# Heads issued in pairs on the matrix engine, and a reordered last block, in a fused two-block transformer kernel

## The chip, the cores and the metric

The kernel runs as one program on one core of a Trainium2 chip. The metric is device time in microseconds (us), lower is better. TensorE (PE in the profile) multiplies matrices, VectorE (DVE), ScalarE (ACT) and GpSimd (POOL) work elementwise, SyncE (SP) starts the DMA transfers. The engines run side by side and meet only at semaphores. A wait stops everything behind it on its own engine.

## The reference, cut to what matters

512 tokens of width 1024 in float32 go through a first block of two layers, which is not touched, and then through a second block with four branches on the normalised input u:

```python
u = rms_norm(h, norm_mix_pre)
hq, hf, hi, hg, pz, sq, sk, sv, iq, ik, iw, mq = split(u @ w_in)
y_a = hgrn2_mixer(hq, hf, hi, hg, ...)   # gated recurrence, 4 heads, values 64 wide
y_b = pool_mixer(pz, ...)                # trailing-window means
y_c = dsa_mixer(sq, sk, sv, iq, ik, iw)  # indexer, top-128 keys, softmax attention
mk, mv = split(rms_norm(mem, norm_mem) @ w_mem_kv)
y_m = mem_attention(mq, mk, mv)          # 256 memory tokens, 4 heads
merged = sum(sigmoid(u @ w_gate[b]) * (y @ w_branch[b]) for b, y in branches)
h = h + rms_norm(merged @ w_out)         # then a gated feed-forward layer

# the indexer: 8 heads of width 64, weighted sum of relu over heads
logits = einsum('bqhd,bsd->bqsh', iq, ik) * 64 ** -0.5
score = einsum('bqsh,bqh->bqs', relu(logits), iw * 8 ** -0.5)
top_val, top_idx = top_k(score, 128)
```

## The kernel before, in words

Activations lie transposed in SBUF: 128 channels on the partitions, 512 tokens along the free dimension. A weight tile is a 1024 x 128 slice (8 blocks). It passes through four slots: SP loads it to RAW, ACT copies a rounded high part to WH (`hi_ahead`, L361), DVE or POOL writes the rest to WL (`lo_ahead`, `lo_one`, L377 and L367). Each dense product is then three matmuls per block (high x high, low x high, high x low; L397 to L399, in the last block also L1350 to L1352). High parts are made three tiles ahead of their use. Results of tiles alternate between PSUM banks 0 and 1, and PE may use a bank again once `evac` says it was read. A plain float32 matmul shows as two records.

All orders are written out by hand, one instruction list per engine. Four places matter here, all in the second block.

**Memory stage.** `second_pe` first makes memory keys (two tiles, `mem_kv(0)` and `mem_kv(1)`) and memory values (`mem_kv(2)`, `mem_kv(3)`), each 256 columns wide, through banks 0 and 1. PE then waits for both values to be read, and `lin_pair` runs the first two tiles of `w_in` block by block as the normalised input arrives. In `second_dve` the input blocks are scaled (L2553, `rn`) and their low parts made (L2556), ACT makes their high parts (L1942). The two values are read out (`mem_scaled`, L2539) and two weight tiles split between the first input blocks.

**Index loop.** 24 scores (3 query blocks x 8 heads, index r) of 64-row operands, 256, 384 and 512 keys wide (L1378). Even heads lie on partitions 0 to 63, odd heads on 64 to 127. Each goes to bank 2 or 3, ACT applies relu into PR (L1987), and DVE adds it into SC with its weight (L2636, L2639). After each score PE does one piece of filler: 3 matmuls of a gate tile, or after every 8 such pieces a branch product of 6 matmuls (`gated`, `branch_out`). After scores 8 and 17 ACT also handles a gate (`gate_act`: split, tanh, split), DVE after scores 9 and 18 a `merge`. Then DVE selects the top keys in 16 rounds (`select_round`) between further merges, which free banks for the gates and branches on PE.

**Sparse attention.** Eight steps of `pe_attend(("dsa",), ...)` with 11 pieces of 12 further tiles of `w_in` after each step. Step 7's softmax, the tiles' low parts (`LOWS`), the preparation of the recurrence on DVE (`hgrn_prepare`) and its logarithms on ACT (`hgrn_logs`) share the in-order queues. The result of the second pair of heads leaves bank 6 by ACT (`act_out`, L626) and DVE (`dve_out`, L633). Only then can `branch_out(2, 0)` run on PE.

**Recurrence.** Nine levels: DVE makes exponents (`decay`), ACT the exponential, DVE the scaled factors XX (`scale_by`), PE the products (L1431, L1440, L1449), DVE stores them into ATT (`keep`). PE fills with gate pieces. After the last level the values are applied (L1459, `hg_o`): head by head, into partition halves of one bank per pair of heads, 512, 384, 256 and 128 columns wide.

Of the kernel before, what the change touches and what calls it, by code (L numbers as in the profile page):

```python
# [18 lines left out]
P = 128  # L19
T = 512  # L20
D = 1024
DT = D // P
# [49 lines left out]
class Counts:  # L72
# [20 lines left out]
 asum ysum yt yo ot_in xt_in z r_tok merge os brf var_out var_in""".split()  # L93


def program(nc, known, t):
# [3 lines left out]
    with ctx:  # L100
# [758 lines left out]
        M_MQ = M_OUT + 4  # L859
# [316 lines left out]
        def _(pe):  # L1176
# [93 lines left out]
            def second_pe():  # L1270
# [19 lines left out]
                mem_kv(2)  # L1290
                mem_kv(3)
                evac_of(pe, M_MQ - 2)
                evac_of(pe, M_MQ - 1)
                lin_pair(XH, XL, ("r_hi", "r_lo"), "mixpre")
                turn("mv", MVT, 4)
# [77 lines left out]
                for r in range(24):  # L1373
                    qb, ih = r // 8 + 1, r % 8
                    rr = slice(ih % 2 * 64, ih % 2 * 64 + 64)
                    if r >= 2:
                        pe.wait_ge(sem["ixr"], cnt.value("ixr", r - 2))
                    x = pe.matmul(PB[2 + r % 2][:, 0:(qb + 1) * P], IQ[rr, ih // 2, qb * P:qb * P + P], IK2[rr, 0:(qb + 1) * P], start=True, stop=True)  # L1378
                    done(x, "ix", r)
                    next(fill)  # L1380
# [74 lines left out]
                for pr in range(2):  # L1455
                    for e in range(2):
                        h = 2 * pr + e
                        for a in range(TT):
# [305 lines left out]
        def _(act):  # L1764
# [164 lines left out]
            def second_act():  # L1929
# [8 lines left out]
                nxt()  # L1938
                rsqrt_act(act, "mixpre", D, EPS6)
                for j in range(DT):  # L1940
                    act.wait_ge(sem["rn"], cnt.value("rn", ("mixpre", j)))
                    done(act.activation(XH[:, j], ACC[:, j], ACT.Copy), "r_hi", ("mixpre", j))  # L1942
                    if j in (0, 1):
                        hi_ahead(act, st)
                        nxt()
# [23 lines left out]
                def gate_act(br, o):  # L1969
# [12 lines left out]
                    st.n += 1  # L1982
                for r in range(24):
# [21 lines left out]
                def dsa_between(c):  # L2005
                    for k in range(12):
# [22 lines left out]
                    if c == 7:  # L2029
                        hgrn_logs(14)  # L2030
# [203 lines left out]
        def _(dve):  # L2234
# [299 lines left out]
            def second_dve():  # L2534
# [15 lines left out]
                for j in range(DT + 1):  # L2550
# [6 lines left out]
                    if j in (0, 1):  # L2557
                        mem_scaled(MVT[:, j * NMEM:(j + 1) * NMEM])
# [99 lines left out]
                for c in range(2, 16):  # L2658
                    for _ in range(min(2 - c % 2, 16 - rnd)):
# [70 lines left out]
                LOWS = {0: (3,), 1: (4,), 2: (5,), 3: (6, 7), 4: (8,), 5: (9,), 6: (10, 11)}  # L2730
# [268 lines left out]
```

## Time and profile before

| | |
|---|---|
| median of 3 runs | 2342.56 us (2341.58 to 2343.31) |
| profiled execution | 2343.34 us, span 2341.3 us |
| PE busy | 2237.2 us (96%), mean granted clock 0.974 |
| DVE / ACT / POOL busy | 1244.0 (53%) / 888.9 (38%) / 345.5 us (15%) |

PE is a busy row because its matmuls overlap: a record of a 512-column matmul lasts 0.39 us while the next one starts 0.227 us later. So what PE can give back is seen in start times, in the granted clock and in idle times in brackets, not in the busy share. All times of rows are us from the span's start.

### The profile page before, as it was taken

Reading aid. Unit: us, or ns where it says so; the run is one execution under the profiler, and the core shown is the slowest. Engines: PE = TensorE matmul, PEld = TensorE weight load, DVE = VectorE, ACT = ScalarE, POOL = GpSimd, SP = SyncE. Lnnn points to the kernel's source line nnn. Section 1 sums busy time; section 2 is a strip of 40 time slices with the busy share of each in tenths; the row PEclk is TensorE's granted clock in tenths of the full one; section 3 lists DMA queues with packets and bytes.
Section 4 is the critical chain, followed back from the end, with each engine's and each line's share of the span. In section 5 each row is a group of like instructions: output and inputs, shape, how many; then the busy total and the mean of one; then the engine's idle time right before and its main releaser. Section 6 shows DMA issues by size and latency. Waiting matters only on the chain.

```text
span 2341.3 us, 27967 instructions
## 1 busy us (share of the span) xinstructions
PE 2237.2 (96%) x10174; PEld 1751.0 (75%) x10176; DVE 1244.0 (53%) x1936; ACT 888.9 (38%) x1463; POOL 345.5 (15%) x215
## 2 busy tenths in 40 slices
PE   7999899999999998899999989999989997999998
PEld 5767688888777776688888777568768775888886
DVE  4576643343554554643343575278589677443344
ACT  3545442242344553431342444322543343332333
POOL 0000600002410003400002510133023232000001
PEclk9999999999999999999999999779999998999999
DMA  5113233333232232233333333123222141323322
GB/s 165 24 44 93 64 100 110 89 96 99 72 110 73 73 99 64 72 102 104 90 99 99 90 100 83 32 64 102 74 59 73 48 115 55 99 85 112 90 73 71
DMA packets 368849, 196.90 MB, mean 84 GB/s; under 512 B 21072, under 2 KB 363869, under 8 KB 368750
## 3 DMA queue, kind: packets, MB, share of 16 engines
q1 hardware_dynamic: 368750, 195.58, 29.3%
q8 instruction: 62, 1.02, 0.2%
q14 instruction: 37, 0.30, 0.0%
HBM read 193.40 MB, written 2.14 MB: 84 GB/s over the span
## 4 chain that ended last, share of the span: by engine, by line
PE 86%; DVE 7%; ACT 3%; issue 2%; SPq 1%; DMA 0%; POOL 0%; DVEq 0%; ACTq 0%; POOLq 0%
PE PB L397 21%; PE PB L399 21%; PE PB L398 21%; PE PB L1350 3%; PE PB L1351 2%; PE PB L1352 2%; PE PB L480 2%; PE PB L526 2%; PE PB L499 2%; PE PB L1378 1%; PE PB L1431 1%; PE PB L1258 1%; PE PB L1259 1%; DVE WL L367 1%; PE PB L1264 1%
## 5 line engine op out<-in xcount | busy, mean ns | idle before, releaser
L361 ACT ACTIVATE WH<-RAW 128x1024 fp32r<-128x1024 f32 (+2 forms) x367 | 369.6, 1011 | 387.5 <-PE PB L399 359.5
L397 PE MATMUL PB<-XH,WH 128*128 128x512 f32 x1248 | 493.1, 395 | 12.7 <-DVE WL L367 6.6
L399 PE MATMUL PB<-XH,WL 128*128 128x512 f32 x1248 | 487.9, 391 | 0.0
L398 PE MATMUL PB<-XL,WH 128*128 128x512 f32 x1248 | 487.7, 391 | 0.0
L377 DVE TENSOR_TENSOR WL<-RAW,WH 128x1024 fp32r<-128x1024 f32 x192 | 252.6, 1316 | 187.2 <-ACT WH L361 177.0
L397 PEld LDWEIGHTS PB<-XH,WH 128*128 128x128 f32 x1248 | 235.1, 188 | 65.8 <-issue 12.4
L399 PEld LDWEIGHTS PB<-XH,WL 128*128 128x128 f32 x1248 | 235.0, 188 | 50.4
L398 PEld LDWEIGHTS PB<-XL,WH 128*128 128x128 f32 x1248 | 235.1, 188 | 47.9
L399 PE MATMUL PB<-HH,WL 128*128 128x512 f32 x512 | 199.2, 389 | 0.0
L397 PE MATMUL PB<-HH,WH 128*128 128x512 f32 x512 | 199.2, 389 | 0.0
L398 PE MATMUL PB<-HL,WH 128*128 128x512 f32 x512 | 199.2, 389 | 0.0
L367 DVE TENSOR_TENSOR WL<-RAW,WH 128x1024 fp32r<-128x1024 f32 (+3 forms) x135 | 167.0, 1240 | 58.2 <-ACT WH L361 57.8
L367 POOL TENSOR_TENSOR WL<-RAW,WH 128x1024 fp32r<-128x1024 f32 (+1 forms) x48 | 104.9, 2192 | 365.9 <-ACT WH L361 324.5
L765 POOL TENSOR_TENSOR SM<-ACC 128x512 f32<-128x512 f32 x4 | 5.2, 1292 | 895.9 <-DVE ACC L2409 530.8
L1871 ACT ACTIVATE HS<-HR 128x512 f32<-128x512 f32 x64 | 40.5, 632 | 195.2 <-DVE HR L2427 195.2
L613 ACT ACTIVATE PT<-PB 128x256 f32<-128x256 f32 (+3 forms) x160 | 65.4, 411 | 128.7 <-PE PB L499 128.7
L399 PEld LDWEIGHTS PB<-HH,WL 128*128 128x128 f32 x512 | 96.1, 188 | 20.1
L397 PEld LDWEIGHTS PB<-HH,WH 128*128 128x128 f32 x512 | 96.1, 188 | 19.9
L398 PEld LDWEIGHTS PB<-HL,WH 128*128 128x128 f32 x512 | 96.1, 188 | 19.8
L1350 PE MATMUL PB<-XH,WH 128*128 128x512 f32 x256 | 108.2, 423 | 1.0 <-ACT RS L1978 1.0
L1352 PE MATMUL PB<-XH,WL 128*128 128x512 f32 x256 | 103.6, 405 | 0.0
L1351 PE MATMUL PB<-XL,WH 128*128 128x512 f32 x256 | 103.6, 405 | 0.0
(506 smaller groups left out, 3624.8 us busy)
## 6 DMA issues: line engine op xcount, KB each, us to landing
RAW<-in_w_up SPq DMA_DIRECT2D x64, 512.0 KB, 4.1
RAW<-in_w_down SPq DMA_DIRECT2D x64, 512.0 KB, 3.8
RAW<-in_w_ffn_gate_up SPq DMA_DIRECT2D x44, 512.0 KB, 3.7
RAW<-in_w_gate SPq DMA_DIRECT2D x32, 512.0 KB, 3.9
RAW<-in_od_w_in SPq DMA_DIRECT2D x24, 512.0 KB, 6.2
RAW<-in_w_in SPq DMA_DIRECT2D x24, 512.0 KB, 3.7
RAW<-in_ple_w_gate SPq DMA_DIRECT2D x16, 512.0 KB, 4.0
RAW<-in_w_ffn_down SPq DMA_DIRECT2D x16, 512.0 KB, 3.8
```

Source lines behind the costliest of these rows:

```text
L361: act.activation(WH[:, s, 0:nb], RAW[:, s, 0:nb], ACT.Copy).then_inc(hi_done[s], 1)
L367: eng.tensor_tensor(WL[:, s, 0:nb], RAW[:, s, 0:nb], WH[:, s, 0:nb].bitcast(F32), ALU.subtract).then_inc(lo_done[s], 1)
L377: dve.tensor_tensor(WL[:, s], RAW[:, s], WH[:, s].bitcast(F32), ALU.subtract).then_inc(lo_done[s], 1)
L397: pe.matmul(PB[b][0:m, 0:n], WH[:, s, k, 0:m], rh[:, kk, :], start=kk == 0, stop=False)
L398: pe.matmul(PB[b][0:m, 0:n], WH[:, s, k, 0:m], rl[:, kk, :], start=False, stop=False)
L399: x = pe.matmul(PB[b][0:m, 0:n], WL[:, s, k, 0:m], rh[:, kk, :], start=False, stop=kk == last)
L480: xs[e] = pe.matmul(PB[2 + e][:, lo:lo + w], q[:, qb * P:qb * P + P], k[:, ks[0] * P:ks[0] * P + w], start=True, stop=plain)
L499: x = pe.transpose(PB[4 + e][:, c * P:c * P + P], PR[:, e, c * P:c * P + P], ID[:])
L613: done(act.activation(PT[:, e, ks[0]:ks[0] + len(ks), qb * P:qb * P + P], PB[4 + e][:, 0:len(ks) * P].rearrange("p (j q) -> p j q", q=P), ...
L1350: pe.matmul(PB[m % 2][:], WH[:, n % 4, k], XH[:, k], start=k == 0, stop=False)
L1351: pe.matmul(PB[m % 2][:], WH[:, n % 4, k], XL[:, k], start=False, stop=False)
L1352: x = pe.matmul(PB[m % 2][:], WL[:, n % 4, k], XH[:, k], start=False, stop=k == DT - 1)
```

## The change

It touches the second block alone. The memory values go into the two halves of PSUM bank 2 and DVE reads them in one instruction after the input blocks; PE waits for that (`mvt`) ahead of their transposition. Four splits of weight tiles move with it. The index loop issues two heads together, waits for both relus of the pair before, and runs two pieces of filler after them. In `hg_o` the two heads of a pair take turns block by block. The exp/tanh table is loaded ahead of the index loop and directly after the logarithms of step 5. The tanh of the recurrence moves ahead of the last copies out of step 7. The first merge after the index loop comes before the first selection rounds. Low parts of tiles 6 and 10 are made one step earlier, and the second `dve_out` comes before the first product of the recurrence.

```diff
--- before.py
+++ after.py
...
@@ -856,7 +856,7 @@
         M_IN = 2
         M_OUT = M_IN + 12 + 16 + 16 + 48 + 2 + 8
         M_OUT += 1 + 24 + 8 + 48 + 2 + 8
-        M_MQ = M_OUT + 4
+        M_MQ = M_OUT + 2
         M_GATE = {3: M_MQ + 12, 1: M_MQ + 28, 2: M_MQ + 56, 0: M_MQ + 72}
 
         def gate_bank(br, o):
@@ -1287,11 +1287,19 @@
                 mem_kv(0)
                 mem_kv(1)
                 pe_misc(pe, ("var", "mixpre"), x_squares)
-                mem_kv(2)
-                mem_kv(3)
-                evac_of(pe, M_MQ - 2)
-                evac_of(pe, M_MQ - 1)
+                pe.wait_ge(sem["pj_free"], cnt.value("pj_free", (1, 5)))
+                for c in range(2):
+                    s, u = st.slot(0)
+                    pe.wait_ge(lo_done[s], u + 1)
+                    into = PB[2][:, c * NMEM:(c + 1) * NMEM]
+                    for k in range(DT):
+                        pe.matmul(into, WH[:, s, k], MH[:, k], start=k == 0, stop=False)
+                        pe.matmul(into, WH[:, s, k], ML[:, k], start=False, stop=False)
+                        x = pe.matmul(into, WL[:, s, k], MH[:, k], start=False, stop=k == DT - 1)
+                    x.then_inc(used[s], 1)
+                    st.n += 1
                 lin_pair(XH, XL, ("r_hi", "r_lo"), "mixpre")
+                pe.wait_ge(sem["mvt"], cnt.value("mvt", 0))
                 turn("mv", MVT, 4)
                 for c in range(2):
                     lin1(8, XH, XL)
@@ -1370,13 +1378,17 @@
                 pe.wait_ge(sem["score_free"], cnt.value("score_free", 143))
                 pe.wait_ge(sem["score_free"], cnt.value("score_free", 142))
                 fill = itertools.chain(gated(3), gated(1))
-                for r in range(24):
-                    qb, ih = r // 8 + 1, r % 8
-                    rr = slice(ih % 2 * 64, ih % 2 * 64 + 64)
-                    if r >= 2:
-                        pe.wait_ge(sem["ixr"], cnt.value("ixr", r - 2))
-                    x = pe.matmul(PB[2 + r % 2][:, 0:(qb + 1) * P], IQ[rr, ih // 2, qb * P:qb * P + P], IK2[rr, 0:(qb + 1) * P], start=True, stop=True)
-                    done(x, "ix", r)
+                for pair in range(12):
+                    qb, it = pair // 4 + 1, pair % 4
+                    w = (qb + 1) * P
+                    if pair:
+                        pe.wait_ge(sem["ixr"], cnt.value("ixr", 2 * pair - 2))
+                        pe.wait_ge(sem["ixr"], cnt.value("ixr", 2 * pair - 1))
+                    for e in range(2):
+                        rr = slice(e * 64, e * 64 + 64)
+                        x = pe.matmul(PB[2 + e][:, 0:w], IQ[rr, it, qb * P:qb * P + P], IK2[rr, 0:w], start=True, stop=True)
+                        done(x, "ix", 2 * pair + e)
+                    next(fill)
                     next(fill)
                 for _ in fill:
                     pass
@@ -1453,9 +1465,9 @@
                 pe.wait_ge(sem["hg_read"], cnt.value("hg_read", q - 1))
                 pe.wait_ge(sem["misc_free"], cnt.value("misc_free", ("hv", 1)))
                 for pr in range(2):
-                    for e in range(2):
-                        h = 2 * pr + e
-                        for a in range(TT):
+                    for a in range(TT):
+                        for e in range(2):
+                            h = 2 * pr + e
                             x = pe.matmul(PB[6 - 4 * pr][e * 64:e * 64 + 64, a * P:T], HV[:, a, h * 64:h * 64 + 64],
                                           ATT[:, h, SLOT[a]:SLOT[a] + TT - a, :], start=a == 0, stop=a == TT - 1)
                     done(x, "hg_o", pr)
@@ -1936,13 +1948,14 @@
                 nxt()
                 hi_ahead(act, st)
                 nxt()
+                hi_ahead(act, st)
+                st.n += 1
                 rsqrt_act(act, "mixpre", D, EPS6)
+                hi_ahead(act, st)
+                st.n += 1
                 for j in range(DT):
                     act.wait_ge(sem["rn"], cnt.value("rn", ("mixpre", j)))
                     done(act.activation(XH[:, j], ACC[:, j], ACT.Copy), "r_hi", ("mixpre", j))
-                    if j in (0, 1):
-                        hi_ahead(act, st)
-                        nxt()
                 for c in range(2):
                     copy_out(MQ[:, c], scale=-0.125)
                 for c in range(2):
@@ -1980,6 +1993,7 @@
                         st.n += 1
                     hi_ahead(act, st)
                     st.n += 1
+                act.preload_act_table_set("exp_and_others")
                 for r in range(24):
                     w = (r // 8 + 2) * P
                     act.wait_ge(sem["ix"], cnt.value("ix", r))
@@ -2003,6 +2017,8 @@
                         done(act.activation(ACC[:, 0:4], ACC[:, 4:8], ACT.Tanh, scale=0.5), "hg_e", "tanh")
 
                 def dsa_between(c):
+                    if c == 7:
+                        hgrn_logs(14)
                     for k in range(12):
                         if (8 * k + 10) // 11 - 1 != c:
                             continue
@@ -2026,8 +2042,7 @@
                         done(act.activation(KK[:], KK[:], ACT.Exp, scale=-1.0), "hg_e", "inv")
                     if c == 5:
                         hgrn_logs(9)
-                    if c == 7:
-                        hgrn_logs(14)
+                        act.preload_act_table_set("exp_and_others")
                 act.preload_act_table_set(LN_TABLE)
                 act_attend(act, ("dsa",), 2, dsa_between, lambda: copy_out(ACC[:, 0]))
 
@@ -2554,8 +2569,15 @@
                     if j:
                         dve.wait_ge(sem["r_hi"], cnt.value("r_hi", ("mixpre", j - 1)))
                         done(dve.tensor_tensor(XL[:, j - 1], ACC[:, j - 1], XH[:, j - 1].bitcast(F32), ALU.subtract), "r_lo", ("mixpre", j - 1))
-                    if j in (0, 1):
-                        mem_scaled(MVT[:, j * NMEM:(j + 1) * NMEM])
+                    if j == 0:
+                        lo_ahead(dve, st)
+                        st.n += 1
+                lo_ahead(dve, st)
+                lin_ready(dve, st)
+                st.n += 1
+                twice = MRB[0][:].unsqueeze(1).to_broadcast([P, 2, NMEM])
+                halves_of = PB[2][:].rearrange("p (c n) -> p c n", n=NMEM)
+                done(dve.tensor_tensor(MVT[:].rearrange("p (c n) -> p c n", n=NMEM), halves_of, twice, ALU.mult), "mvt", 0)
                 for c in range(2):
                     skip()
                 dve.wait_ge(sem["misc"], cnt.value("misc", "mv"))
@@ -2656,7 +2678,7 @@
                     dve.wait_ge(sem["topk"], cnt.value("topk", (r, TT - 1, 1)))
                 rnd = 0
                 for c in range(2, 16):
-                    for _ in range(min(2 - c % 2, 16 - rnd)):
+                    for _ in range({2: 0, 3: 2}.get(c, min(2 - c % 2, 16 - rnd))):
                         select_round(rnd)
                         rnd += 1
                     merge(3 if c < DT else 1, c % DT)
@@ -2727,7 +2749,7 @@
                             for k in range(blk + n + 1, blk + 2 * n):
                                 link(dve.tensor_tensor(OFF[:, lv, :, k], OFF[:, 0, :, k - 1], OFF[:, lv, :, k - 1], ALU.add))
                 PREPARED = {3: (0,), 4: (1, 5), 5: (6, 7, 8), 6: (10, 11), 7: (14,)}
-                LOWS = {0: (3,), 1: (4,), 2: (5,), 3: (6, 7), 4: (8,), 5: (9,), 6: (10, 11)}
+                LOWS = {0: (3,), 1: (4,), 2: (5, 6), 3: (7,), 4: (8,), 5: (9, 10), 6: (11,)}
 
                 def dsa_between(c):
                     for n in LOWS.get(c, ()):
@@ -2741,8 +2763,8 @@
                         hgrn_prepare(12)
                         hgrn_prepare(13)
                 dve_attend(dve, ("dsa",), 2, dsa_between, last=False)
+                dve_out(dve, "dsa", 1)
                 dve.wait_ge(sem["hg_e"], cnt.value("hg_e", "tanh"))
-                dve.wait_ge(sem["pv"], cnt.value("pv", 19))
                 done(dve.scalar_tensor_tensor(QQ[:], ACC[:, 0:4], 1.0, ACC[:, 4:8], ALU.add, ALU.mult), "hg_small", "qk")
 
                 def halves(t_, lv):
@@ -2801,7 +2823,6 @@
                     done(x, "hg_read", q)
                     dve.wait_ge(sem["hg_read"], cnt.value("hg_read", q))
                 decay(0)
-                dve_out(dve, "dsa", 1)
                 for lv in range(9):
                     scale_by(lv)
                     if lv < 8:
```

## Rows read from the trace of the kernel before

**Rows 1.** The page, chain that ended last: shares of the span by engine.
```profile
PE 86%; DVE 7%; ACT 3%; issue 2%; SPq 1%; DMA 0%; POOL 0%; DVEq 0%; ACTq 0%; POOLq 0%
```

**Rows 2.** Stretches: us, busy us per engine (x instructions), PE clock, DMA share, GB/s.
```profile
1370.00:1404.00 34.00, 27.77 (x158) 24.03 (x157) 23.46 (x36) 15.02 (x21) 2.06 (x4) 0.90 0.31 85
...
1510.00:1520.00 10.00, 10.00 (x16) 3.99 (x15) 1.72 (x3) 1.58 (x3) 0.00 (x0) 0.50 0.01 2
...
1543.00:1560.00 17.00, 17.00 (x63) 13.46 (x63) 15.78 (x35) 5.26 (x7) 6.06 (x4) 0.84 0.16 46
...
1760.00:1800.00 40.00, 40.00 (x237) 35.32 (x236) 38.84 (x40) 15.10 (x14) 12.31 (x7) 1.00 0.24 66
```

**Rows 3.** Timeline of the memory stage: start, us, engine, line, [idle before <-releaser].
```profile
1383.45 0.75 DVE L2553 SCALAR_TENSOR_TENSOR ACC<-X,VEC,RS 128x512 f32<-128x512 f32 x1
...
1391.63 0.77 PE L1258 MATMUL PB<-XH,WH 128*128 128x512 f32 x1 [6.22 <-DVE MVT L2539]
...
1392.45 0.75 DVE L2553 SCALAR_TENSOR_TENSOR ACC<-X,VEC,RS 128x512 f32<-128x512 f32 x1
...
1393.71 0.75 DVE L2553 SCALAR_TENSOR_TENSOR ACC<-X,VEC,RS 128x512 f32<-128x512 f32 x1
...
1404.22 0.60 PE L1183 MATMUL PB<-ID,MVT 128*128 128x128 f32 x4
```

**Rows 4.** Timeline of PE in the index loop, 256 and 384 keys.
```profile
1480.74 0.70 PE L1378 MATMUL PB<-IK,IQ 64*128 64x256 f32 x2
...
1481.37 0.50 PE L1350 MATMUL PB<-XH,WH 128*128 128x512 f32 x1
...
1482.26 0.70 PE L1378 MATMUL PB<-IK,IQ 64*128 64x256 f32 x2
...
1491.38 0.91 PE L1378 MATMUL PB<-IK,IQ 64*128 64x384 f32 x2
...
1492.22 0.50 PE L1336 MATMUL PB<-YBH,WH 128*128 128x512 f32 x1
```

**Rows 5.** Timeline of PE at the index loop's end, 512 keys.
```profile
1541.17 2.07 PE L1378 MATMUL PB<-IK,IQ 64*128 64x512 f32 x2
1543.17 0.79 PE L1350 MATMUL PB<-XH,WH 128*128 128x512 f32 x1
```

**Rows 6.** Timeline of PE in the memory attention, scores of two heads together.
```profile
1428.96 0.70 PE L480 MATMUL PB<-MK,MQ 64*128 64x256 f32 x4
1429.60 0.66 PE L499 MATMUL PB<-ID,PR 128*128 128x128 f32 x4
```

**Rows 7.** Timeline of the index loop after score 9.
```profile
1493.78 1.28 ACT L1978 ACT_TABLE_LOAD   x1
...
1495.73 0.51 PE L1350 MATMUL PB<-XH,WH 128*128 128x512 f32 x1 [1.01 <-ACT RS L1978]
```

**Rows 8.** Timeline of the sparse attention's steps 6 and 7.
```profile
1706.34 1.90 ACT L2000 ACTIVATE FC<-FC 128x2048 f32<-128x2048 f32 x1
...
1712.32 0.66 PE L397 MATMUL PB<-XH,WH 128*128 128x512 f32 x1 [4.25 <-DVE WL L367]
...
1720.78 0.63 PE L1183 MATMUL PB<-ID,VT 128*128 128x128 f32 x4 [0.23 <-DVE HV L2739]
```

**Rows 9.** Timeline from the sparse attention into the recurrence.
```profile
1730.83 2.29 DVE L2746 SCALAR_TENSOR_TENSOR QQ<-ACC 128x2048 f32<-128x2048 f32 x1 [2.61 <-ACT ACC L2003]
...
1739.30 0.50 PE L1336 MATMUL PB<-YAH,WH 128*128 128x512 f32 x1 [4.46 <-DVE YAL L633]
...
1745.80 3.73 PE L1431 MATMUL PB<-XX 128*128 128x128 f32 x32
```

**Rows 10.** Timeline of PE after the recurrence's eighth level.
```profile
1823.26 2.02 PE L1440 MATMUL PB<-XX 128*128 128x128 f32 x16 [1.02 <-DVE ATT L2794]
```

**Rows 11.** Timeline of PE, values of the sparse attention, then of the recurrence.
```profile
1726.81 2.37 PE L526 MATMUL PB<-PT,SV 128*64 128x512 f32 x16
...
1840.95 7.05 PE L1459 MATMUL PB<-ATT,HV 128*64 128x512 f32 x32
```

More of the change, by code:

```diff
@@ L92 @@
  topk hsp hg_x hg_prod hg_read hg_e hg_d hg_o hg_small hx mn m2 varb ln_v x_full sum7q pj pj_free memsum cross xsum
- asum ysum yt yo ot_in xt_in z r_tok merge os brf var_out var_in""".split()
+ asum ysum mvt yt yo ot_in xt_in z r_tok merge os brf var_out var_in""".split()
 def program(nc, known, t):
```

## The prediction, made before the changed kernel was run

> **What bounds the kernel.** I read the chain of waits first: PE carries 86% of the path to the end [rows 1], so a gain must shorten PE's own work, raise its clock or close a hole in it. The stretches of the second block come next [rows 2]. In 1370 to 1404 PE is busy 27.77 of 34 us at a mean clock of 0.90: a hole. In 1510 to 1520 it is busy all the time at 0.50, that is at 1.2 instead of 2.4 GHz: a slow clock. In 1760 to 1800 PE shows 40.00 and DVE 38.84 busy us: two engines at their limit. The timelines of these places give the terms. The first block isn't touched, and elsewhere PE runs without holes, so a shift there is passed on rigidly.
>
> **Memory stage.** PE stands 6.22 us until DVE has read the second value tile, restarts at 1391.63 with a slow clock (0.77 us for a record) and reaches the transposition at 1404.22 [rows 3]. The change takes the values out of banks 0 and 1. What PE waits for next is the low part of the second `w_in` tile. DVE makes it straight after the first input block: 1383.45 + 0.75 + 1.23 (my reading of such a split; the table of groups has 1.24) = 1385.4. From there DVE gives one input block each 1.26 us (1392.45 to 1393.71), while PE needs six matmuls of 0.227 = 1.36 us per block; high parts come 1.4 us after the start of their scaling. PE takes four matmuls, waits 0.4 us for block 1 at 1386.75, and then is the limit: 7 x 1.36 + 0.45 = 10.0, end at 1396.75. DVE ends the eighth low part at 1395.1, splits one tile (1.2) and reads the values in one 512-wide instruction (0.7): 1397.0. So the new wait costs 0.25 us and the transposition starts at 1397.0 instead of 1404.22: **7.2 us**. Two moved splits on ACT fall into gaps (one ahead of the inverse root, one while DVE computes it); if one delays the first high part, it costs at most its 1.05 us. If PE were slowed through the whole pair I would lose the 48 matmuls' 0.2 us for about 3.4 us, some 1.7. I take 7.2, ends 4.5 and 8.
>
> **Index loop.** At full clock a 256-wide score takes 0.63 us of PE's time (1480.74 to 1481.37) and a piece of filler 0.89 (to 1482.26), of which 3 x 0.227 = 0.68 are matmuls and 0.21 the change of shape. At 384 it is 0.84, at 512 by the same step 1.05 [rows 4]. Two heads of the memory attention on the two row halves, also 256 wide, take 0.64 together [rows 6]: a second head is free. So a pair costs one score and two pieces cost 0.21 + 1.36 = 1.57: periods of 2.2, 2.4 and 2.6 us.
> Does the wait for both relus bind? After a pair ACT needs 0.1 + 0.5 + 0.6 = 1.2 to 1.35 us even at 512, under 1.57. DVE's two sums take 1.5 in a period of 2.6. It binds at two places. The table load of 1.28 us [rows 7] now stands before the first relu: PE waits 0.55. After score 8 ACT's split, tanh and split stand before relu 9. The second piece after that pair needs the tanh, 2.1 us after the pair, and PE is there at 1.57: 0.5, and again 0.3 for relu 9. Before, the hole at this place was 1.01 in PE and ended by the tanh behind the load [rows 7].
> Sum from the first score at 1479.22 (1480.74 less one period of 1.52): 2.8 + 3 x 2.2 + 3.95 + 3 x 2.4 + (1.05 + 0.21 + 0.68 + 1.36, with a branch product) + 3 x 2.6 = 31.7 us. Before, the last piece starts at 1543.17 [rows 5] and ends 1.45 later: 65.4 us. That is 33.7. Most is clock: a 512-wide score takes 2.00 us [rows 5] instead of 1.05, in a loop that stays at 0.50 [rows 2]. I assume the fall does not happen. It came after the hole of 1.01 us, in a loop where half of PE's rows idle in each score. The new loop uses all rows, and its period at 512 is 60% filler against 36 to 45%. After the loop the old kernel stays slow a little: 0.84 over 17 us [rows 2] is 5.4 us at 1.2 GHz, 3.8 of them after the loop, nine matmuls that lose 0.2 each: 1.8. Together **35.5 us**, ends 18 (slow clock, below) and 37.
> Selection: DVE is busy 15.78 of 17 us while PE never idles [rows 2]. The merge put before the first rounds frees the bank earlier, and the two rounds it displaces (3.1 us each) are caught up by the next merge, about 3 us before PE wants it. Nothing, at worst 1 us.
>
> **Sparse attention.** The low part of tile 10 leaves its place behind step 7's softmax, and the hole of 4.25 us before 1712.32 [rows 8] closes. But 1.15 us of splitting and 1.28 us of table load are now ahead of that softmax, behind logarithms that end at 1708.24 [rows 8]. Its probabilities come 2.4 us later. PE waits about 2 us for them, then for the next thing that is late: the second transposition of recurrence values needs DVE's copy of the first, which was the last waiter already (0.23 at 1720.78). That copy comes 2.4 later less the 1.15 of the split that left: 1.3 us later. The hole moves; it does not go. The values then end 1.3 us later, `dve_out` (0.7) comes next, and the first product of the recurrence starts near 1732.3 instead of 1730.83 [rows 9].
> Here the table load has two prices. In the row, 1.28 us, the next activation starts at once. The Trainium skill, "ScalarE: Activation LUTs", What ACT_TABLE_LOAD costs, adds 1.38 us of drain, 2.66 in all. By that rule each moved load would cost 1.4 more in its chain, and the sum would be some 2 us smaller. No drain is seen here, so the row's price stands in the sum.
>
> **Start of the recurrence.** The 4.46 us hole before 1739.30 [rows 9] ends because the low part of the output no longer waits behind two long DVE operations. PE reaches the first level's product near 1741, but the factors XX, before at 1743.0, now come 1.5 us later. From there DVE is full (38.84 of 40 [rows 2]), and at the eighth level PE waits 1.02 us for it [rows 10]. So PE's lead is lost and only DVE's start counts: minus 1.5, plus about 1 of DVE's waits for the late first product at 1745.80 [rows 9]. This stage together: **0.5 us lost**, ends 3 lost and 6 gained.
>
> **Recurrent values.** The same shapes for one pair of heads in turns are there: 16 records in 2.3 us. Head by head, 32 records take 7.05 [rows 11]. Two pairs in turns: 4.55. Everything to the end of the branch (sums of squares, roots, high and low parts) follows the last of these. **2.5 us**, ends 1.5 and 2.7.
>
> **Sum.** 7.2 + 35.5 - 0.5 + 2.5 = 44.7. From the profiled execution's 2343.34 us that gives 2298.6; its own time is 0.8 above the median of the runs, so 2298 us. Other edits (tile 6 one step earlier, tanh before copies) lie beside a PE without holes: nothing.
>
> **Rivals.**
> 1. The clock falls in the index loop all the same, say at the disturbed fifth pair, 13.4 us in. For it: the fall before came there, and the loop never recovered. Against: twice the rows in use, more filler. At half clock a pair takes 1.57, 2.00 and its filler 2.86: 3 x 4.4 + 6.1 + 3 x 4.9 = 34 us after the 13.4. The loop gives 18 instead of 33.7, the tail nothing: 44.7 - 17.5 = 27: 2316 us.
> 2. The pairs do not overlap, since scores here have other operands per half. Against: rows 6. Each pair then costs 0.43, 0.64 or 0.85 more, 4 of each: 7.7 us: 2306.
> 3. The sparse attention keeps what it closes (softmax earlier than I think, or DVE with slack in the levels): 6 more: 2292.
> 4. Slower than before: scores one after the other and a clock that is slow from the first pair, because 4 records of half the rows follow each other. Periods are then 5.1, 6.0 and 6.9, four of each, plus 2.6 for the branch products: 74.6 against 65.4. It decides from a mean clock of about 0.55 in the loop. Lost 9.2, with the memory stage's 7.2 back and nothing from the values: 2345.
> 5. The memory stage gives nothing, as PE waits for the one late read instead: 2305. It would need the input blocks to come 7 us later than computed.
>
> **Chances.** Forecast 0.72 (own range 2293 to 2303), rival 1 0.11, rival 2 0.04, rival 3 0.09, rival 4 0.02, rival 5 0.02. The range 2290 to 2312 takes in the unknown ends, rivals 2, 3 and 5 and a clock that falls late. About 0.2% (4.7 us) is what can be told from no change: faster 0.97, same 0.02, slower 0.01.
>
> **What would show it.** Memory stage: first `w_in` matmul near 1385.5, transposition near 1397, clock 1.00. Index loop: clock 1.00, pairs of four records in 0.64 to 1.05 us, 32 us in all. Step 7: PE holes near 2 and 3 to 4 us instead of 4.25; `branch_out(2, 0)` without a hole, a new one before the first level's product, DVE without waits through the levels. Values of the recurrence: 32 records in 4.5 us. The prediction is wrong if the loop's clock is below 0.9, or if PE's lead of the sparse attention survives the eighth level.

## The result and the profile after

| | before | after |
|---|---|---|
| median of runs (us) | 2342.32 (2341.58 to 2343.31, 4 runs) | 2306.80 (2303.79 to 2307.34, 4 runs) |
| ratio | | 0.9845, 95% interval 0.9828 to 0.9863 |
| profiled execution, its span | 2343.34, 2341.3 | 2307.16, 2305.1 |
| mean granted clock | 0.974 | 0.984 |

The change saves 35.5 us, where 44 were forecast. First the profile page's chain of waits, to be laid beside [rows 1]: PE has lost 2 points of the path, DVE has gained 1 and "issue" 2.

```profile
PE 84%; DVE 8%; issue 4%; ACT 3%; SPq 1%; DMA 0%; POOL 0%; DVEq 0%; ACTq 0%; POOLq 0%
```

Stretches of the kernel after, with the columns of [rows 2]. The memory stage has PE busy 33.80 of 34 us at clock 1.00 (27.77 at 0.90 before), the index loop runs at 1.00 where it was at 0.50. Behind a hole in the sparse attention the clock is 0.66. In the first levels of the recurrence DVE is busy 39.21 of 40 us and PE no longer 40.00 but 38.44.

```profile
1370.00:1404.00 34.00, 33.80 (x190) 28.54 (x189) 27.87 (x40) 18.31 (x25) 2.15 (x5) 1.00 0.41 112
1490.00:1500.00 10.00, 10.00 (x41) 5.66 (x39) 5.22 (x9) 5.52 (x10) 1.16 (x1) 1.00 0.19 54
1510.00:1520.00 10.00, 10.00 (x45) 8.26 (x45) 9.76 (x25) 2.61 (x3) 3.47 (x2) 1.00 0.26 79
1680.00:1690.00 10.00, 7.62 (x27) 6.32 (x28) 9.55 (x19) 3.86 (x4) 2.85 (x2) 0.66 0.05 13
1705.00:1745.00 40.00, 38.44 (x233) 33.96 (x234) 39.21 (x39) 14.90 (x14) 11.13 (x5) 1.00 0.17 48
```

Timeline of PE after, the starts that answer to [rows 3], [rows 7 to 11]: transposition of the memory values; a pair of scores at 256 keys (0.70 us for four records); the last pair, behind a hole; two holes that stand where one of 4.25 us was, and the slow restart behind the second; the first level; the eighth; the recurrent values, which begin at 1808.18.

```profile
1398.46 0.60 PE L1183 MATMUL PB<-ID,MVT 128*128 128x128 f32 x4
...
1478.58 0.70 PE L1389 MATMUL PB<-IK,IQ 64*128 64x256 f32 x4
...
1504.32 1.13 PE L1389 MATMUL PB<-IK,IQ 64*128 64x512 f32 x4 [1.42 <-ACT PR L2001]
...
1672.77 0.66 PE L499 MATMUL PB<-ID,PR 128*128 128x128 f32 x4 [1.09 <-DVE PR L604]
...
1682.38 1.09 PE L1183 MATMUL PB<-ID,VT 128*128 128x128 f32 x4 [5.83 <-DVE HV L2761]
1683.12 0.78 PE L397 MATMUL PB<-XH,WH 128*128 128x512 f32 x1
1683.70 0.63 PE L398 MATMUL PB<-XL,WH 128*128 128x512 f32 x1
...
1705.33 3.84 PE L1443 MATMUL PB<-XX 128*128 128x128 f32 x32 [2.08 <-DVE XX L2807]
...
1788.88 3.49 PE L1452 MATMUL PB<-XX 128*128 128x128 f32 x16 [1.92 <-DVE ATT L2816]
...
1808.18 4.53 PE L1471 MATMUL PB<-ATT,HV 128*64 128x512 f32 x32
```

Stage by stage, each as the distance between the same two instructions in both traces:

| from, to | before | after | gain | predicted |
|---|---|---|---|---|
| start, last untouched place before the memory stage | 1377.78 | 1379.42 | -1.6 | 0 |
| from there to the transposition | 26.44 | 19.04 | 7.4 | 7.2 |
| to the first index score | 75.00 | 75.07 | -0.1 | 0 |
| to the first sparse score (loop and tail) | 158.69 | 124.55 | 34.1 | 35.5 |
| sparse attention, to the second block of its values [rows 11] | 88.90 | 92.37 | -3.5 | } |
| to the first level's product | 18.99 | 14.88 | 4.1 | } -0.5 |
| to the eighth level's product | 77.46 | 83.55 | -6.1 | } |
| to the recurrent values | 17.69 | 19.30 | -1.6 | } |
| to the end | 500.35 | 496.92 | 3.4 | 2.5 |

The sum is 36.2, the difference of the spans. The first row is code that the change doesn't touch.

One pattern stands behind the 6.1 and 1.6 us lost in the levels. Timelines of DVE and then of POOL in the second and third level of the kernel after: DVE's subtraction, 1.23 us elsewhere, takes 3.29 us beside a split of POOL that reads two tiles from SBUF, and ends 1.08 us after it. XX at 1723.26 and 1725.24 is stretched in the same way.

```profile
1713.17 1.22 DVE L2807 TENSOR_TENSOR XX<-EE,QQ 128x1024 f32<-128x1024 f32 x1
1714.43 3.29 DVE L2784 TENSOR_TENSOR EE<-FC 128x1024 f32<-128x1024 f32 x1
1717.64 1.21 DVE L2785 TENSOR_TENSOR EE<-FC 128x1024 f32<-128x1024 f32 x1
...
1723.26 2.05 DVE L2806 TENSOR_TENSOR XX<-EE,KK 128x1024 f32<-128x1024 f32 x1
1725.24 2.31 DVE L2807 TENSOR_TENSOR XX<-EE,QQ 128x1024 f32<-128x1024 f32 x1
```
```profile
1713.83 2.81 POOL L367 TENSOR_TENSOR WL<-RAW,WH 128x1024 fp32r<-128x1024 f32 x1 [11.74 <-ACT WH L361]
1721.82 4.64 POOL L367 TENSOR_TENSOR WL<-RAW,WH 128x1024 fp32r<-128x1024 f32 x2 [5.19 <-ACT WH L361]
```

### The profile page after: what moved, and what is told of

Its sections match the earlier page's. It is cut to its first block, busy times and chain, and to the rows that moved or that the text cites. A ratio compares the mean times of both kernels' runs of the same rounds, so it can differ in the third digit from the quotient of the medians.

```text
span 2305.1 us, 27976 instructions
## 1 busy us (share of the span) xinstructions
PE 2201.5 (96%) x10174; PEld 1738.3 (75%) x10176; DVE 1251.2 (54%) x1935; ACT 888.0 (39%) x1463; POOL 347.6 (15%) x215
## 4 chain that ended last, share of the span: by engine, by line
PE 84%; DVE 8%; issue 4%; ACT 3%; SPq 1%; DMA 0%; POOL 0%; DVEq 0%; ACTq 0%; POOLq 0%
PE PB L397 22%; PE PB L399 21%; PE PB L398 21%; PE PB L480 2%; PE PB L526 2%; PE PB L1358 2%; PE PB L1360 2%; PE PB L1359 2%; PE PB L499 2%; DVE ATT L2816 1%; PE PB L1258 1%; PE PB L1259 1%; PE PB L1264 1%; DVE XX L2807 1%; PE PB L1344 0%
## 5 line engine op out<-in xcount | busy, mean ns | idle before, releaser
L398 PE MATMUL PB<-XL,WH 128*128 128x512 f32 x1248 | 488.2, 391 | 0.0
L2444 DVE TENSOR_TENSOR HL<-HS,HH 128x512 f32 x64 | 44.3, 692 | 106.9 <-ACT HH L1885 106.9
```

The lines of the kernel that those rows point to most:

```text
L398: pe.matmul(PB[b][0:m, 0:n], WH[:, s, k, 0:m], rl[:, kk, :], start=False, stop=False)
```

## The experiments

Times are medians; "after" is 2306.8, and each run stands beside runs of the kernel before on its own chip (36 of them in four batches, 2338.3 to 2346.5, medians of the batches 2342.5 to 2343.4). Executions of one kernel lie 1 to 7 us apart where the clock does not differ. Part of that arises ahead of the first edit: the last untouched place before the memory stage is reached between 1376.7 and 1380.4 us in the traces. So differences of 2 us between two kernels say little.

### What made the clock fall in the index loop

**Scores one by one, early table load kept.**
```
-for pair in range(12): ...        (two heads, two fillers)
+for r in range(24):               (one head, one filler)
+    if r >= 2: pe.wait_ge(sem["ixr"], cnt.value("ixr", r - 2))
```


> The changed kernel with its index scores one by one again, a wait and one filler piece behind each; all else as changed, the early table load too. Theory: a score of half of PE's rows between single pieces of filler brings the clock to 1.2 GHz by itself, with or without the hole of 1.01 us: the loop's granted clock falls to 0.50 to 0.60, the loop takes about 63 us instead of 32, and the time is 30 to 34 us above the changed kernel's, about 2338. Rival: the hole alone set off the fall, and the early load takes it away: the clock stays near 1.00; 12 further scores at full clock (4 each of 0.63, 0.84, 1.05) are 10 us, so about 2317.


Measured 2317.66 (2316.17 to 2318.59), ratio to before 0.9891 [0.9876, 0.9906]. My theory fell, the rival's number came: half-row scores between single fillers, with no hole among them, kept the clock at 1.00 in this trace. The pairing alone is worth 10.9 us by the medians and 9.6 in the traces' stage of loop and tail (134.10 against 124.55), which the rival worked out as 12 scores that no longer take time, 10 us.

**The kernel before with the early table load only.**
```
+act.preload_act_table_set("exp_and_others")
 for r in range(24):
```


> The kernel before with one edit, the exp table loaded ahead of its index loop. Theory: the hole of 1.01 us before 1495.73 goes, the clock falls all the same to 0.50 some us later, since scores and filler are the same; time within 3 us of before (2342). Rival: the hole was what set off the fall: clock near 1.00 through the loop, 25 to 30 us faster, about 2315.


Measured 2326.78 (2326.48 to 2328.06), 0.9932 [0.9916, 0.9947]: 16 us faster by one instruction that moved. The clock did what the rival said, the time lies between the two numbers. Stretches of this trace: the clock is 1.00 where it was 0.50 [rows 2], and falls only behind a new hole.

```profile
1510.00:1520.00 10.00, 10.00 (x29) 4.47 (x28) 6.34 (x7) 4.47 (x7) 2.38 (x1) 1.00 0.18 52
1520.00:1530.00 10.00, 10.00 (x40) 7.08 (x39) 7.47 (x13) 3.26 (x5) 3.70 (x2) 1.00 0.15 44
1530.00:1540.00 10.00, 6.59 (x22) 4.93 (x22) 9.83 (x25) 2.60 (x3) 1.80 (x1) 0.83 0.11 34
```
The hole, in this trace's timeline of PE, with the record at 0.63 instead of 0.39 us behind it:

```profile
1534.97 0.50 PE L1336 MATMUL PB<-YBH,WH 128*128 128x512 f32 x1 [3.41 <-DVE RS L2623]
...
1537.61 0.63 PE L1352 MATMUL PB<-XH,WL 128*128 128x512 f32 x1
```
PE, faster now, waits for two selection rounds and a merge on DVE. From the first index score to the first sparse score this trace takes 139.43 instead of 158.69 us, 19.3 less. With the hole of 3.41 and eight matmuls that lose 0.2 us each behind it that is 24.3, near the 25 that a fall costs (below). From 19.3 down to 16 it is a later start of the untouched code (1.1) and the sparse attention up to the first level (1.6).

**Pairs without the early table load.** (`preload_act_table_set` ahead of the loop taken out.)


> The changed kernel without the early exp table load, so that the 1.28 us load stands again between two activations of the fifth pair. Theory: the two heads of a score keep the clock at 1.00 even with a hole of 1 to 1.5 us there; the 0.5 us hole at the first pair goes, so the time is 0 to 2 us above the changed kernel's (2307 to 2309). Rival: the hole sets off the fall in this loop too: clock 0.50 from about 13 us in, 15 us or more slower, 2322 or above.


Measured 2305.17 (2304.61 to 2307.49), ranges that overlap with after's. The price of the theory, 0 to 2 us slower, isn't seen in the median; loop and tail take 125.40 instead of 124.55. The hole is there, and longer than the one of [rows 7]:

```profile
1484.37 0.50 PE L1358 MATMUL PB<-XH,WH 128*128 128x512 f32 x1 [1.84 <-ACT RS L1991]
```
and the two stretches around it stay at full clock:
```profile
1480.00:1490.00 10.00, 8.13 (x34) 4.56 (x33) 4.59 (x9) 6.00 (x10) 3.61 (x2) 1.00 0.29 79
1490.00:1500.00 10.00, 10.00 (x40) 5.21 (x39) 5.31 (x6) 4.53 (x8) 2.38 (x1) 1.00 0.01 2
```
**Neither: single scores, no early load, all else as after.**


> The changed kernel with both its index loop edits undone: scores one by one and no early exp table load, all else as changed. So far, in the same surroundings: pairs with the early load 2306.8, pairs without it 2305.2, single scores with it 2317.7, and the clock at 1.00 in all three. Theory (a hole and half-row scores slow the clock only together): the hole of about 1 us behind the table load stands between single scores again, the clock falls to 0.50 behind it and stays there to the loop's end, and the time is 20 us or more above that of single scores with the early load, 2336 to 2342. Rival (the fall of the kernel before had a cause outside the loop): the clock stays at 1.00 and the time is that of single scores with the load plus or minus 2, about 2318.


The five executions took 2341.59, 2317.53, 2318.78, 2314.58 and 2315.28 us. A median says nothing here: the kernel has two outcomes, the theory's once and the rival's four times. The profile is of the first, and there the clock goes right behind the 1.01 us hole:

```profile
1490.23 0.50 PE L1358 MATMUL PB<-XH,WH 128*128 128x512 f32 x1 [1.01 <-ACT RS L1987]
```
```profile
1490.00:1500.00 10.00, 9.77 (x19) 4.48 (x20) 4.13 (x6) 2.55 (x6) 1.96 (x2) 0.62 0.26 79
1500.00:1510.00 10.00, 10.00 (x17) 4.00 (x16) 1.86 (x3) 1.47 (x3) 0.00 (x0) 0.50 0.00 0
```
The first lies 25 us above the mean of the other four (2316.5): the price of a fall. With the hole and the half-row scores together a fall is possible, not certain; in these five it came once. All 36 runs of the kernel before had a mean clock of 0.971 to 0.977, against 0.984 to 0.986 in the four here that did not fall. What in the surroundings makes it certain there stays open; up to the hole the scores of both kernels start equally far apart (1.52 us).

This limits what the other runs show. In the kernel before, the early load alone kept the clock (4 executions without a fall, against 36 with one). In the surroundings of the kernel after, a fall is rare even with both loop edits undone, so five executions of pairs without the load, and four of single scores with it, could have escaped it by luck. That the pairs alone would hold the clock is not shown, and the other edits of the change have a part in it that no run separates.

**Selection rounds dealt out as before.** (`{2: 0, 3: 2}.get(c, ...)` back to `min(...)`.)


> The changed kernel with the selection rounds dealt out among the merges as before (one or two ahead of the first two merges too). In the kernel before with the early table load, where the clock stayed at 1.00, PE stood 3.41 us behind the index loop until DVE had done two rounds and the merge. Theory: the same hole comes back here, and PE restarts on a slow clock behind it (0.63 us for a record instead of 0.39): 3.5 to 5 us slower, 2310 to 2312. Rival: the loop of pairs ends otherwise, DVE's two rounds fit beside the filler: within 1 us of 2306.8, as the prediction had it.


Measured 2313.17 (2311.08 to 2314.20), 0.9870 [0.9854, 0.9885]: the theory's hole and a little more than its price, 6.4 slower, 5.4 of it between the first index score and the first sparse score (129.96 against 124.55). The hole is the same:

```profile
1516.83 0.50 PE L1344 MATMUL PB<-YBH,WH 128*128 128x512 f32 x1 [3.49 <-DVE RS L2644]
```

### The memory stage

**Old memory stage in the kernel after** (value tiles in banks 0 and 1, two reads by DVE).


> The changed kernel with the old memory stage (value tiles in banks 0 and 1, read after the first two input blocks). Theory: a rigid shift, PE again stands about 6.2 us for DVE's second read and restarts on a slow clock; 7.4 us slower, 2314, from the transposition on everything later by the same. Rival: part of the gain was lost again downstream, so that undoing it costs less than 5 us.


Measured 2313.78 (2313.43 to 2314.43): 7.0 slower. Nothing of this gain is lost downstream.

### Where the sparse attention and the levels lost

**All of these edits undone.**
```
-LOWS = {0: (3,), 1: (4,), 2: (5, 6), 3: (7,), 4: (8,), 5: (9, 10), 6: (11,)}
+LOWS = {0: (3,), 1: (4,), 2: (5,), 3: (6, 7), 4: (8,), 5: (9,), 6: (10, 11)}
```
and the tanh behind the copies of step 7, no table load behind step 5, `dve_out` behind `decay(0)`.


> The changed kernel with every edit of the sparse attention and the recurrence's start undone (order of the tanh, table load behind step 5, low parts of tiles 6, 7, 10, 11, place of the output read). Theory: these edits cost 3.5 us in the sparse attention and 7.7 in the levels and the start of the values, and bring 4.1 before the first level's product; undone, the time is 5 to 7 us below the changed kernel's, 2300 to 2302, with the 4.25 and 4.46 us holes back and PE waits of under 2 us in the levels. Rival: the levels' loss comes from what is not undone here (how the loop's earlier end sets the transfers and POOL's splits), so that only the 3.5 and the 4.1 exchange: about 2307 or slower.


Measured 2298.12 (2297.85 to 2301.20), 0.9815 [0.9802, 0.9828]: 8.7 below after and the fastest complete kernel of this study. In the traces 6.6 of it lie between the first sparse score and the ninth level; 2.7 are an earlier start of untouched code. From the first level's product to that of the ninth it takes 85.48 us, to the hundredth what it took before, against 93.18 after. Groups of DVE over the levels, first after, then this kernel (the mean of one is the number after "|" and the comma):

```profile
L2807 DVE TENSOR_TENSOR XX<-EE,QQ 128x1024 f32<-128x1024 f32 x8 | 14.1, 1764 | 0.0
L2806 DVE TENSOR_TENSOR XX<-EE,KK 128x1024 f32<-128x1024 f32 x8 | 12.3, 1537 | 0.3
```
```profile
L2805 DVE TENSOR_TENSOR XX<-EE,KK 128x1024 f32<-128x1024 f32 x8 | 9.8, 1226 | 0.3
L2806 DVE TENSOR_TENSOR XX<-EE,QQ 128x1024 f32<-128x1024 f32 x8 | 9.8, 1219 | 0.0
```
In this trace POOL's splits fall elsewhere. DVE, then POOL, in the second level; the merge takes 2.17 instead of 0.69 us:

```profile
1708.32 1.23 DVE L2805 TENSOR_TENSOR XX<-EE,KK 128x1024 f32<-128x1024 f32 x1
...
1713.70 2.17 DVE L2648 SCALAR_TENSOR_TENSOR MG<-GT,MG 128x512 f32<-128x512 f32 x1
1715.80 3.08 DVE L2815 COPY_PREDICATED ATT<-LMASK,PB 128x512 f32<-128x512 int32 x4
```
```profile
1712.09 3.24 POOL L367 TENSOR_TENSOR WL<-RAW,WH 128x1024 fp32r<-128x1024 f32 x1 [17.08 <-ACT WH L361]
1716.04 2.38 POOL L367 TENSOR_TENSOR WL<-RAW,WH 128x1024 fp32r<-128x1024 f32 x1 [0.72 <-ACT WH L361]
```
**The same edits one by one.** Output read behind the first decay again:


> The changed kernel with the sparse attention's second output read on DVE after the query product and the first decay, as before; tanh, table load and low parts as changed. Theory: the hole of 4 us or so before that output's products comes back, and DVE starts the levels some 2.3 us earlier; since DVE is the limit in the levels, the end of the levels moves with DVE, and the time is 0.7 us (one output read less ahead of them) to 3 us below the changed kernel's, 2304 to 2306. Rival: PE's hole is passed on to the end: 2 to 4 us slower, 2309 to 2311.


2305.43 (2299.75 to 2306.58): the theory's number, but 1.4 below after is within the spread; the rival is out. The levels still take 92.12.

Only the tanh order and the load behind step 5 undone:


> The changed kernel with only the tanh order and the table load behind step 5 of the sparse attention undone; low parts of the tiles and the output read as changed. With all of these edits undone the time was 2298.1. Theory: the load (1.28 us) and the tanh path delayed the seventh softmax and with it the copy of the second value tile (5.83 us hole); undone here, the sparse attention and the start of the levels get shorter and DVE starts its levels some 3 us earlier: 2299 to 2303. Rival: the place of the low parts is what costs: within 1.5 us of the changed kernel's 2306.8.


2307.10 (2305.02 to 2307.64): no difference, so my account of this part, a late softmax, fails. The softmax is earlier, but two DVE instructions right behind it now take it back, and PE's wait for the value copy grows to 8.87 us. DVE, then POOL, in this trace:

```profile
1674.34 4.48 DVE L2725 TENSOR_TENSOR ACC<-ACC,FC 128x2048 f32<-128x2048 f32 x1
1678.85 5.38 DVE L2729 TENSOR_TENSOR_SCAN FC<-TMP,ACC 128x512 f32<-128x512 f32 x2
```
```profile
1673.59 9.56 POOL L367 TENSOR_TENSOR WL<-RAW,WH 128x1024 fp32r<-128x1024 f32 x3 [84.31 <-ACT WH L361]
```
In after the same two take 4.47 and 2.34 us. From the second level on, the levels run as in the kernel before (88.15 in all), which makes up for the late start.

Only the low parts back in their places:


> The changed kernel with only the low parts of tiles 6, 7, 10 and 11 back in their old places; tanh order, table load and output read as changed. Theory (the table load ahead of the late softmax costs, the low parts do not): the low part of tile 10 stands behind a softmax that is 2.4 us late, so PE's hole before step 7 is 6 to 7 us instead of 1.1 and 5.8 in two, and nothing is won: 2306 to 2310. Rival (the low parts cost): 2299 to 2303.


2302.29 (2301.42 to 2302.63), 4.5 below after: the rival again. The hole of 5.67 us before step 7 is back, but it replaces 1.09 and 5.83. The sparse attention gains 2.0 (90.32 against 92.37) and the levels 1.5; 1.8 are an earlier start of untouched code.

### The price of POOL beside DVE

```
-for n in range(N_GATE[2] + 3, N_GATE[0] + 12): lo_one(pool, n)
+    pool.tensor_tensor(WL[:, s, 0:1], RAW[:, s, 0:1], WH[:, s, 0:1]..., ALU.subtract)
```


> The changed kernel with POOL's splits beside the recurrence's levels cut to one block of eight: the low parts of the gate and merge tiles in this stretch are left out but for their first block (2.4 us of POOL become about 0.3 each). Theory: DVE's two-operand instructions on SBUF in the levels (1.58 and 1.84 us mean for XX, against 1.22 in the kernel before) are stretched by POOL's at the same time; without them each takes 1.2, DVE's busy time in the levels falls by 5 us or more, PE's waits for XX go, and the time is 5 to 8 us below the changed kernel's, 2299 to 2302. Rival: the instructions are slow for another reason (their own operands, ScalarE), and the time stays within 1.5 us of 2307.


This kernel leaves out seven of eight blocks of these low parts, so it only measures. 2295.77 (2293.82 to 2296.77), 11.0 below after, more than the theory's 5 to 8. The levels take 84.33 instead of 93.18 us, and XX is back at its length in this trace's groups, with POOL's splits at 0.76 us each instead of 2.60:

```profile
L2808 DVE TENSOR_TENSOR XX<-EE,KK 128x1024 f32<-128x1024 f32 x8 | 9.8, 1225 | 0.3
L2809 DVE TENSOR_TENSOR XX<-EE,QQ 128x1024 f32<-128x1024 f32 x8 | 9.7, 1218 | 0.0
```
```profile
L1156 POOL TENSOR_TENSOR WL<-RAW,WH 128x128 fp32r<-128x128 f32 x12 | 9.1, 761 | 77.1 <-ACT WH L361 67.0 <-ACT WH L2066 10.1
```
### A step further

The sparse edits undone, and `dve_out(dve, "dsa", 1)` between the query product and `decay(0)`:


> The kernel with the sparse edits undone (2298.1) and one new step: the sparse attention's second output is read on DVE between the query product and the first decay. In the trace of that kernel YAH is there at 1688.7, before the query product ends at 1690.6, so DVE waits for nothing, PE's hole of 4.46 us before the output's products goes, and the factors of the first level come 0.7 us later (1701.1 instead of 1700.4). PE, without the hole, would be at the first product by 1699.3 and waits for them till about 1701.2. Theory: the first product comes 2.5 us earlier (1701.2 instead of 1703.7) and some of it lasts to the end of the levels, since DVE's waits there grow less: 0.5 to 2.5 us faster, 2295.6 to 2297.6. Rival: the shift moves POOL's splits onto DVE's two-operand instructions again, as in the changed kernel (levels 93 us instead of 85.5), and the time is 3 us or more above 2298.1.


Measured 2302.55 (2299.95 to 2303.42): slower by 4.4 than without the step. The theory's first half came: the 4.46 us hole went, and from the first sparse score to the first level's product it took 105.20 instead of 108.36 us. Then the levels took 91.69 instead of 85.48, 6.2 given back for 3.2 won; 1.35 of the rest is a later start of the two traces' common code. Groups of this trace:

```profile
L2807 DVE TENSOR_TENSOR XX<-EE,QQ 128x1024 f32<-128x1024 f32 x8 | 14.1, 1764 | 0.0
L2806 DVE TENSOR_TENSOR XX<-EE,KK 128x1024 f32<-128x1024 f32 x8 | 12.3, 1543 | 0.3
```
So the levels have two patterns. In the quick one (before, before with the early load, sparse edits undone, tanh order undone: 85.5, 85.5, 85.5, 88.2) in every second level POOL's first split starts 3.8 us after the first XX; the splits fall on a merge (2.17 instead of 0.69 us), on reads of PSUM and, in the levels between, on an EE (2.20 instead of 1.23). In the slow one (after, output read undone, low parts undone, this kernel: 93.2, 92.1, 91.7, 91.7) they start 1.4 us before it or 1.8 us behind and fall on XX (2.05 and 2.31) and EE (3.29). The five other kernels that keep the sparse edits are slow too (91.6 to 93.2). Each pattern repeats itself from level to level once begun.

## Why the prediction was right, and where it failed

- **Direction and size.** 2306.8 lies in the range 2290 to 2312, 8.8 above the forecast and outside its own range of 2293 to 2303. The times of rivals 2 (2306) and 5 (2305) were met by accident: the pairs do overlap, and the memory stage gave its 7 us.
- **Memory stage, 7.2.** 7.4 in the trace, 7.0 undone. Less the 1.64 us by which this trace is late, the first `w_in` matmul starts at 1385.6 and the transposition at 1396.8, where 1385.5 and 1397 were forecast.
- **Index loop, 35.5.** 34.1. The 1.4 that lack are the hole of 1.42 us before the last pair: ScalarE waited for a sum of DVE that took 2.43 us instead of 0.75 beside a split of POOL (lines of DVE, then of POOL, below). I had counted ACT and DVE as free at 512 keys from durations alone.

```profile
1499.33 2.43 DVE L2661 SCALAR_TENSOR_TENSOR SC<-PR,IWT,SC 128x512 f32<-128x512 f32 x1 [1.99 <-ACT PR L2001]
```
```profile
1498.84 2.37 POOL L367 TENSOR_TENSOR WL<-RAW,WH 128x1024 fp32r<-128x1024 f32 x1 [9.43 <-ACT WH L361]
```
- **Why the clock held.** I gave two reasons, no 1.01 us hole and full rows, leant on the second and set rival 1 on "the clock falls all the same". The first is shown for the kernel before, where the early load alone kept the clock; the second is not shown. Single scores with the early load stayed at 1.00, and so did pairs with a hole of 1.84 us, but with both edits undone the clock fell in only one execution of five. So the clock held, as forecast, and whether it held for my reasons is in part open. Of the 34 us, about 10 are the free scores; a fall costs 25.
- **Selection rounds, "nothing".** Right as a term, since PE has no hole there, but without this edit the quick loop runs into 3.49 us of waiting and a slow restart, 6.4 in all. The sum gave the edit no price, and it is part of the 34.1.
- **Sparse attention, levels and their end, -0.5.** Measured -7.1: this is the step that failed, 6.6 of the 8.5 us by which the sum was too large. Two terms were missing.
  - Slow restart. "The hole moves; it does not go" was right: 4.25 us became 1.09, 0.39 and 5.83, and the transposition behind the last comes 1.4 us later (84.30 us behind the first sparse score instead of 82.87), where 1.3 were forecast. But the second block of the values comes 3.5 us later, not 1.3. Behind the 5.83 us hole PE's matmuls start 0.43 us apart and not 0.227, until 1686.7. From the transposition to the values PE takes 8.07 us instead of 6.03. In the kernel before, the slow restart came behind the 4.25 us hole, at 1712.32, and ahead of another wait, so that it cost nothing. With the low parts alone put back it is again 6.03.
  - Levels. "PE's lead is lost and only DVE's start counts" was right, but the sum kept DVE's work in the levels at its length of before. DVE is as full as it was (39.21 of 40 us against 38.84), yet needs longer for a level, because POOL's splits fall on XX and EE: the levels grew by 7.7. My end of the range for this stage, 3 lost, had no row behind it for that, although the trace of before had EE at 1.71 us mean next to 1.22 in its twin.
- **Recurrent values, 2.5.** 7.05 us became 4.53 (1808.18 to 1812.71), as computed; the stage to the end gave 3.4. No run undoes this edit alone. From the values to the end the two traces with the old order take 500.4 us, the twelve with the new one 496.6 to 498.8, so 2.5 fits and the rest is spread.

In the second level DVE's instruction that reads two tiles of SBUF looks as if it stood still while POOL's split ran: it ended 1.08 us after the split's end at 1716.64, and takes 1.22 alone. POOL, which had begun 0.56 us before the previous XX ended, took 2.81 instead of 2.37 (the split at 1498.84). Copies that read PSUM beside a split kept their length (3.08 to 3.13 us for four). The Trainium skill, "SBUF — State Buffer", SBUF: two separate sides, says that a DVE instruction with two SBUF inputs and a GpSimd instruction that reads SBUF share a port pair as an exclusive lock, and that the one that comes second waits for the whole of the other. The traces agree in both directions, with the 1.08 us of DVE and the 0.44 us more of POOL.

An estimate that the trace of before allowed, and that I did not make: POOL's split took 2.38 us there (at 1758.14). One such split in each of seven levels falling on DVE, less DVE's slack of 1.2 us in 40 [rows 2], is about 14 us lost. It would have set a wider low end than 3.

What decides which pattern the levels take is not settled: both a PE that arrives early and one that arrives late are found with either. That it is a matter of phase, begun in the first two levels, is read from the starts and not shown by a run. Each kernel has one trace, so whether one kernel can show both patterns isn't known. A version that forces the quick pattern (POOL's splits tied to DVE's PSUM reads) was not tried.

## What to carry to other kernels

Before a stage is called "DVE full, so only its start counts", lay POOL's timeline beside DVE's: two-input SBUF instructions of both add up, and moving either by 2 us can cost more than the hole that the move closed. Price a hole with the slow restart behind it, and ask whether another wait absorbs that restart or not. A hole of 1 us on PE can be worth far more than its length: taking the table load out of the loop of the kernel before gave 16 us, for one line. And when a stage gets faster, the next engine's queue order (here two selection rounds ahead of a merge) must be moved in the same step, or part of the gain (6.4 us here) comes back as waiting.

## What the runs showed of the hardware that I had not expected

- A fall of the clock can be a matter of chance: same kernel, same chip, 2341.6 once and 2314.6 to 2318.8 four times.
- A hole of 1.84 us in the loop of pairs left the clock at 1.00; behind one of 1.01 us between single half-row scores it went to 0.50 for the rest of the loop (one trace each).
- The same slow restart cost 2.0 us where it stood behind PE's last wait of a stretch, and nothing where another wait followed.
- A DVE scan pair grew from 2.34 to 5.38 us beside three splits of POOL, whose own mean was then 3.2 us instead of 2.4.
